# Token-order products of a two-block transformer kernel: weight chunks as halves of the contraction, 512 columns at a time

## The reference

```python
# hybrid layer
x = x + 0.5 * swiglu(rms_norm(x, ffn1_norm), ffn1_w_gate_up, ffn1_w_down)
z = rms_norm(x, mix_norm) @ w_in          # pool input, q, k, v, two gates
y_attn = moba_attention(q, k, v)          # v: 256 tokens x 512
...
# second block's layer
z = x @ w_in                              # q, k, v; retention q, k, v (1024), g; two gates
ya = neighbourhood_attention(q, k, v, rpb)
yb = bidirectional_retention(q_r, k_r, v_r, g_r, ...)
```

## Time and profile before

| | before |
|---|---|
| median of 3 runs | 2016.22 us |
| the profiled execution, in all | 2017.38 us |
| its span, first to last instruction | 2015.6 us |
| mean granted TensorE clock | 0.996 |
| TensorE matmul / weight load busy | 1999.3 / 1875.9 us |
| VectorE / ScalarE / GpSimd busy | 1366.1 / 1042.4 / 190.2 us |
| HBM read | 353.14 MB |

### The profile page before, as it was taken

One profiled execution on the slowest core, in us unless ns is written; L12 is line 12 of the kernel. 1 busy time (PEld: TensorE's weight loads), 2 busy tenths in 40 slices (PEclk: granted clock), 3 DMA queues, 4 the chain that ended last, 5 costly groups with the idle time before them and its releaser, 6 DMA issues.

```text
span 2015.6 us, 35431 instructions
## 1 busy us (share of the span) xinstructions
PE 1999.3 (99%) x14470; PEld 1875.9 (93%) x14470; DVE 1366.1 (68%) x1637; ACT 1042.4 (52%) x1239; POOL 190.2 (9%) x153
## 2 busy tenths in 40 slices
PE   9999999999999999999999999999999999999998
PEld 8999999999999999999999999999999999998997
DVE  7666666766766666677666655677778656577776
ACT  5445555544544455654445644456555553456554
POOL 0000130000000004003004012040002203000000
PEclk9999999999999999999999999999999999999999
DMA  8554534555455555455545544555553544454542
GB/s 298 187 186 169 188 147 168 188 187 187 167 191 185 186 175 177 151 184 215 182 185 189 168 153 161 186 207 188 187 182 135 186 166 147 169 190 166 190 185 83
DMA packets 54131, 359.85 MB, mean 179 GB/s; under 512 B 6416, under 2 KB 7824, under 8 KB 11664
## 3 DMA queue, kind: packets, MB, share of 16 engines
q1 hardware_dynamic: 49536, 348.97, 48.6%
q10 hardware_dynamic: 3904, 5.25, 0.9%
q0 software_dynamic: 592, 4.19, 0.5%
HBM read 353.14 MB, written 1.05 MB: 176 GB/s over the span
## 4 chain that ended last, share of the span: by engine, by line
PE 95%; DVE 2%; ACT 1%; issue 1%; POOL 0%; DMA 0%; POOLq 0%; ACTq 0%; SPq 0%; DVEq 0%
PE gate_two L1605 12%; PE up_two L1605 11%; PE bank L1552 10%; PE bank L1553 10%; PE bank L1554 10%; PE gate_two L1552 8%; PE gate_two L1553 8%; PE gate_two L1554 8%; PE gate_two L1607 6%; PE up_two L1607 6%; PE bank L1701 1%; PE up_two L1732 1%; PE up_two L1716 1%; PE bank L1978 1%; DVE w_lo L978 1%
## 5 line engine op out<-in xcount | busy, mean ns | idle before, releaser
L978 DVE TENSOR_TENSOR w_lo<-raw,w_hi 128x2048 fp32r<-128x2048 f32 x320 | 739.8, 2313 | 221.3 <-ACT w_hi L556 221.0
L556 ACT ACTIVATE w_hi<-raw 128x2048 fp32r<-128x2048 f32 x320 | 609.6, 1905 | 49.2 <-PE bank L1554 41.4
L1605 PE MATMUL gate_two<-br_parts,w_hi 128*128 128x512 f32 x1056 | 378.0, 400 | 2.0 <-DVE w_lo L1151 2.0
L1605 PE MATMUL up_two<-br_parts,w_hi 128*128 128x512 f32 x1024 | 364.7, 399 | 0.3 <-DVE w_lo L978 0.2
L1552 PE MATMUL gate_two<-br_parts,w_hi 128*128 128x256 f32 x1056 | 303.6, 287 | 0.0
L1554 PE MATMUL gate_two<-br_parts,w_hi 128*128 128x256 f32 x1056 | 298.7, 283 | 0.0
L1553 PE MATMUL gate_two<-br_parts,w_lo 128*128 128x256 f32 x1056 | 298.6, 283 | 0.0
L1607 PE MATMUL gate_two<-br_parts,w_lo 128*128 128x256 f32 x1056 | 297.2, 281 | 0.0
L1607 PE MATMUL up_two<-br_parts,w_lo 128*128 128x256 f32 x1024 | 287.7, 281 | 0.0
L1553 PE MATMUL bank<-hid_hi,w_lo 128*128 128x256 f32 x960 | 271.6, 283 | 0.0
L1552 PE MATMUL bank<-hid_lo,w_hi 128*128 128x256 f32 x960 | 271.5, 283 | 0.0
(11 more groups left out here) (268 smaller groups left out, 3217.8 us busy)
## 6 DMA issues: line engine op xcount, KB each, us to landing
raw<-stream SPq DMA_DIRECT2D x328, 1024.0 KB, 4.8
area<-rpb POOLq DMA_DIRECT2D x2, 1536.0 KB, 8.9
raw<-stream SPq DMA_DIRECT2D x8, 256.0 KB, 7.4
softT<-area ACTq DMA_DIRECT2D x32, 64.0 KB, 5.1
konst<-consts SPq DMA_DIRECT2D x1, 1344.0 KB, 9.2
x<-xT ACTq DMA_DIRECT2D x4, 256.0 KB, 6.5
area<-area ACTq DMA_DIRECT2D x8, 128.0 KB, 5.8
ret_turn<-area ACTq DMA_DIRECT2D x8, 128.0 KB, 2.4
```

The source lines that it names most:

```text
L556: act.activation(w_hi[:, s, :], raw[:, s, :], ACT.Copy).then_inc(hi_ready[s], 1)
L978: dve.tensor_tensor(w_lo[:, s, :], raw[:, s, :], w_hi[:, s, :].bitcast(F32), ALU.subtract).then_inc(lo_ready[s], 1)
L1605: pe.matmul(pair[:, f, :, :], w_hi[:, s, at:at + P], parts[:, :, k, :], start=k == 0, stop=False, skip_group_check=True)
```

## The change

The 2048 numbers to a partition of two neighbouring token-order chunks are laid out anew. Before, chunk one is 8 tiles of the contraction by the first 256 columns and chunk two the same by the next 256. After, chunk one is the first 4 tiles of the contraction by all 512 columns, and chunk two the last 4 (`_wide`). `wide_tokens` takes the place of `tokens`: with 512 columns at a time it goes through 4 tiles for token tile 0 into bank 4 and for token tile 1 into bank 5, and a pair of chunks keeps both banks open (`start` in part 0, `stop` in part 1). Part 0 gets a wait before its first product into bank 5, part 1 signals `wide_half` when bank 4 is complete. ScalarE copies bank 4 after `wide_half`, ahead of its wait for the end of the second chunk, and bank 5 after it, 512 columns each; it copies nothing after the first chunk of a pair. The number of chunks, their size and the other chunks stay.

```diff
+        wide_half = signal("wide_half", 1, 3)
...
                 for m in range(MIX1):
                     c = FFN_CHUNKS + m
+                    if m == 5:
+                        act.wait_ge(rs_ready.sem, here.at(rs_ready, 2))
+                        act.wait_ge(wide_half.sem, here.at(wide_half, 1))
+                        act.activation(v_tok[:, 0, :], flat(banks[4][:, :, :]), ACT.Copy, scale=rs[:, 0:1]
+                                       ).then_inc(mix_evac.sem, 1)
                     chunk_done(here, c)
...
-                    elif m < 6:
-                        if m == 4:
-                            act.wait_ge(rs_ready.sem, here.at(rs_ready, 2))
-                        for a in range(TT):
-                            e = act.activation(v_tok[:, a, (m - 4) * T:(m - 3) * T], bank[:, a, :], ACT.Copy,
-                                               scale=rs[:, a:a + 1])
-                        e.then_inc(mix_evac.sem, 1)
+                    elif m == 5:
+                        act.activation(v_tok[:, 1, :], flat(banks[5][:, :, :]), ACT.Copy, scale=rs[:, 1:2]
+                                       ).then_inc(mix_evac.sem, 1)
...
+                def wide_out(a, g):
+                    out = v_tok[:, a, :] if g == 0 else ret_v[:, a, (g - 1) * 2 * T:g * 2 * T]
+                    act.activation(out, flat(banks[4 + a][:, :, :]), ACT.Copy).then_inc(mix_evac.sem, 1)
+
                 for m in range(MIX2):
+                    if m in (5, 11, 13):
+                        if m == 13:
+                            act.wait_ge(qk_ready.sem, here.at(qk_ready, 4))
+                        g = (0, 1, 2)[(5, 11, 13).index(m)]
+                        act.wait_ge(wide_half.sem, here.at(wide_half, g + 1))
+                        wide_out(0, g)
                     chunk_done(here, m)
...
-            def tokens(c, bank, hi, lo):
+            def wide_tokens(here, c, part, left, count):
 
                 s = c % SLOTS
                 for a in range(TT):
-                    for k in range(DT):
-                        rows, cols = slice(a * P, (a + 1) * P), slice(k * T, (k + 1) * T)
-                        e = product(bank[:, a, :], hi[:, k, rows], lo[:, k, rows], w_hi[:, s, cols], w_lo[:, s, cols],
-                                    start=a == 0 and k == 0, stop=k == DT - 1)
+                    rows = slice(a * P, (a + 1) * P)
+                    if part == 0 and a == 1:
+                        pe.wait_ge(left.sem, here.at(left, count))
+                    for k in range(DT // 2):
+                        cols, t = slice(k * 2 * T, (k + 1) * 2 * T), part * DT // 2 + k
+                        e = product(flat(banks[4 + a][:, :, :]), br_hi[:, t, rows], br_lo[:, t, rows], w_hi[:, s, cols],
+                                    w_lo[:, s, cols], start=part == 0 and k == 0, stop=part == 1 and k == DT // 2 - 1)
+                    if part == 1 and a == 0:
+                        e.then_inc(wide_half.sem, 1)
                 return e.then_inc(w_used[s], 1)
...
-                        tokens(c, bank, br_hi, br_lo)
+                        wide_tokens(here, c, m - 4, qk_sq_ready, 4)
...
-                        tokens(m, bank, br_hi, br_lo)
+                        wide_tokens(here, m, m % 2, mix_evac, m)
...
+def _wide(w, first):
+
+    return [_tile(w, slice(i * D // 2, (i + 1) * D // 2), slice(first, first + 2 * T)) for i in range(2)]
```

More of the change, by code:

```diff
@@ L834, in _ @@
                     elif m < 6:
-                        act.activation(v_tok[:, :, (m - 4) * T:(m - 3) * T], bank[:, :, :], ACT.Copy
-                                       ).then_inc(mix_evac.sem, 1)
+                        if m == 5:
+                            wide_out(1, 0)
                     elif m < 10:
@@ L844, in _ @@
                     elif m < 14:
[L845 to L848, removed]
+                        if m in (11, 13):
+                            wide_out(1, m // 2 - 4)
                     elif m < 18:
@@ L2070, in _stream @@
         chunks += _ffn_chunks(a["ffn1_w_gate_up"][l], a["ffn1_w_down"][l])
-        chunks += _columns(w, 6, 512) + _columns(w, 2) + _columns(w, 8, 2048)
+        chunks += _columns(w, 4, 512) + _wide(w, 1536) + _columns(w, 2) + _columns(w, 8, 2048)
         chunks += [_tile(a["w_branch_pool"][l], slice(None), slice(i * wide, (i + 1) * wide)) for i in range(2)]
@@ L2077, in _stream @@
         w = a["w_in_2"][l]
-        chunks += _columns(w, 22)
+        chunks += _columns(w, 4) + _wide(w, 4 * T) + _columns(w, 4, 6 * T) + _wide(w, 10 * T) + _wide(w, 12 * T)
+        chunks += _columns(w, 8, 14 * T)
         chunks += [_tile(a["w_branch_a_2"][l], slice(None), slice(i * wide, (i + 1) * wide)) for i in range(2)]
```

## The result

The changed kernel takes 2012.52 us (median of 21 runs), beside 2016.30 for the one before on the same chips (median of 21): a ratio of 0.998 with an interval of 0.9974 to 0.9986, 2.8 to 5.2 us less. It is faster beyond its interval, by 3.8 us between the medians, which is just under the 4.0 us that the prediction had set as the line. One run of each kernel lies far off, in a slow state (2128.77 and 4611.34 us), and the ratio is taken without them. The profiled executions are 4.4 us apart in their span, 2015.6 and 2011.2.

The account below looks back on a forecast made before the run. The prediction took TensorE's own stream as the bound. From the median of 2016.2 us it subtracted 2.4 us (16 chunks at 0.15), with waits and ScalarE's work at nothing and the clock left to the range: 2013.8 us, range 2009.3 to 2015.8.

Parts of the forecast that it names:

- the line: Whole kernel: two measurements can be told apart from about 0.2%, 4.0 us, on; faster 0.33, same 0.64, slower 0.03.
- The bound: TensorE, busy 99% of the span: time cut from its own stream counts in full; no wait to be won.
- The pace before: Token-order chunks: 256-column products start 0.120 us apart, so 48 take 5.76 us a chunk.
- The pace after: New 512-column products: 0.2337 us each, 5.61 a chunk, saving 0.15; 2.4 over 16 chunks; wrong outside 0.230 to 0.237.
- the pair's excess over the columns: Gate and up chunks, 512- and 256-column products alternating: 0.033 us above the floor, 0.020 of it the wide one's.
- Rival A: New products: fixed price per matmul, wide ones at 0.227 us or less (up to 0.230 counts), 5.1 us saved; chance 0.34.
- the forecast: New 512-column products at 0.230 to 0.237 us, time 2012.2 to 2015.8 us; chance 0.52.
- The doubt about two runs and one: Pair's wide operand is two runs of 256, the new one a run of 512; so below 0.2337 us not excluded.
- The page's rule: Matmul gap N/2.4 + 2.5 ns: halving the matmuls of the changed chunks is worth 1.0 us in all, not measurable.
- The waits: TensorE's new wait before bank 5 and ScalarE's moved bank 4 copy: all met, cost nothing, least spare time 1.4 us.
- Rival C: ScalarE's bank 4 copy holds TensorE at chunks 6, 12 and 14: 4.1 us lost, 2017.9 us; chance 0.04.
- The clock: Half-speed stretch at the first layer's last norm: work comes 1.5 us earlier; 0.75 us either way if clock steps stay.

Follow-up runs that it names:

- e5: Kernel before the change with its 768 token-order products made 384, 320 or 448 columns wide instead of 256; one run, 2065.33 us.
- e3: Changed kernel with each gate or up chunk's 16 products of 512 columns first, its 16 of 256 after them; 2003.92 us, ratio to before 0.9936.
- e1: Changed kernel with the gate and up chunks' 512-column products reading one run of 512 instead of two of 256; 2012.74 us, ratio to before 0.9979.
- e2: Changed kernel with wide chunks' weights laid out so each new 512-column product reads two runs of 256 instead of one of 512; one run, 2012.83 us.

## Why the prediction came out as it did

**The bound.** Right: TensorE's own stream was the bound, no wait was won or lost, and the saving of the chunks (4.46 us) is the saving of the span (4.36). The medians of all runs are closer, 3.8 us apart.

**The pace before.** Right, 0.120. The stretch of the earlier trace rows was misread in a small thing: of its five chunks three are ordinary ones, and the last two, from 1103.36 on, are token-order chunks themselves; both kinds go at 0.120.

**The pace after.** Here the prediction was wrong, by its own sign too: it took 0.2337 and called itself wrong outside 0.230 to 0.237. The mean measured over the new products, a chunk's first interval left out, is 0.228, and 0.2267 once settled. The failed step is the reason given for choosing between the bounds: that the pair's excess over the columns "went mostly with columns". e5 shows at 384 and 320 columns that a product's excess doesn't. The split behind it, 0.120 for the narrow product of a pair and the rest for the wide one, doesn't hold either. The earlier trace rows go on like this:

```profile
97.28 0.28 PE L1607 MATMUL up_two<-br_parts,w_lo 128*128 128x256 f32 x1
97.39 0.40 PE L1605 MATMUL up_two<-br_parts,w_hi 128*128 128x512 f32 x1
97.62 0.28 PE L1607 MATMUL up_two<-br_parts,w_lo 128*128 128x256 f32 x1
97.74 0.40 PE L1605 MATMUL up_two<-br_parts,w_hi 128*128 128x512 f32 x1
```

With the two starts before them, 96.92 and 97.04, the narrow steps are 0.12, 0.11 and 0.12 and the wide ones 0.24 and 0.23: a mean of 0.117 for the narrow, so about 0.2367 for the wide. What stood in place of the step is a fixed price of 0.0133 for each matmul, and in most of the alternating pairs 0.007 more, which e3 shows to go away with grouping. The pair was the nearest row by width and type, but a row of another sequence, and one chunk of many: the up chunk from 374.64, in the same trace, has 0.347 a pair, from which the same subtraction would have given 0.227. The size of the term was 0.15 us a chunk, and it measured 0.28; 16 chunks gave 4.46 us where 2.4 stood.

**Rival A** had the right law (0.0133 a matmul) and the settled value, and by its own band, "up to 0.230", it is the case that came. It gave 5.1 us; the first products of each chunk, slower than settled for five to ten, and one long first interval took 0.6 of that back. It had 0.34 of the chance, the forecast 0.52. The doubt about two runs and one, on which part of A's chance was hung, was idle: e1 and e2.

**The time.** It fell between the two: 2012.52 measured, 2013.8 and 2011.1 foretold. That it lies in the forecast's own range, by 0.3 us, is in part luck. The 4.46 us of the chunks taken from the sum's 2016.2 would be 2011.7, outside it; and the range's lower edge, 2012.2, is not what a pace of 0.230 gives (2016.2 - 3.84 = 2012.4, or 2011.6 with the clock's 0.75 in its favour). The full range, 2009.3 to 2015.8, held the forecast and A both.

**The page's rule.** 0.120 and 0.2267 us from start to start are 11 ns each above the 109.2 and 215.8 ns that were worked out from the Trainium skill's formula for the isolated gap ("TensorE: Matmul & The Clock Gate", section "Back-to-back issue gap"). The same section says that in a stream of weight loads and matmuls the formula counts too little for few columns and too much for many; here it counts too little at 512 columns as well. Its form, columns at 2.4 GHz plus a constant, is borne out at 256, 320, 384 and 512 columns, not at 448; its constant of 2.5 ns is 13.3 here, in products of type fp32r, each with its own weight load.

**The waits.** Right: all met. The least spare time was forecast at 1.4 us and was 1.5. Rival C didn't come, and built on purpose it cost 1.7 us instead of 4.1, because its price let TensorE wait for the second copy too.

**The clock.** The 0.75 us either way was the right size (0.56 and 0.53 at the two norms), but in part by luck. The fear that the clock doesn't move with the work came true at its fall (0.3 us earlier, the work 3.1 us); the length of the slow stretch, which changed as well, and the last norm weren't in the prediction.

## What to carry to other kernels

Where TensorE is the bound, count matmuls beside columns: each one, with its weight load, costs 13 ns here at every width that settled, so 512 columns at half the number of 256 save 5.5% of a settled stretch, and 4.8% of the changed chunks as measured. Keep products of one width together; alternating 512 and 256 columns cost 5 ns a pair more than the same products in groups, and over 2080 pairs that outweighed the change itself. And when an operation's price is taken from a row, look at what stands before and after it there, and at the same row in other places: the price was taken here from a mixed sequence, split by a guess, and a few chunks of the same trace had the other value.

## What the runs showed of the hardware that was not expected

The price of a product depends on what ran before it. After narrow products, wide ones take 0.228 to 0.236 us for about five products and 0.2267 from then on; after wide ones the first narrow one takes 0.113 instead of 0.120 (e3). In some chunks the unsettled start lasts ten products (m = 10, 11 and 13). The width of the neighbours isn't the whole of it, because the same alternating sequence goes at 0.353 us a pair in most chunks and at 0.347 in a few, and not in the same ones in every run. Products of 448 columns settle at 0.0133 above their columns in no chunk seen (mean 0.2035, up to 0.2067 throughout). Whether the 0.0133 belongs to the matmul or to its weight load was not tried: every product here has its own load. What picks the pace of an alternating chunk, how long the settling takes, and what keeps 448 from it, is open.
